# Spreading the gates' running maximum to 128 partitions through memory

## What is computed

```
x += 1/2 * post1(SwiGLU_1(pre1(x)))
x +=       postM(W_out[ mLSTM heads | S5 groups | short-conv channels ](preM(x)))
x += 1/2 * post2(SwiGLU_2(pre2(x)))
```

```
bt = cumsum(log_sigmoid(fg)); dmat[t, s] = bt[t] - bt[s] + ig[s]     (s <= t)
mt = max(max_s dmat[t, s], bt[t] + m)
w  = exp(dmat - mt);   sqk = (q k^T) * w;   num = sqk v + exp(inter - mt) * C q
```

## Time and profile before

| | before |
|---|---|
| median of the timed runs | 1109.81 us |
| the profiled execution, its own time | 1105.96 us |
| its span | 1103.2 us |
| TensorE busy | 1086.5 us (98%) |
| DVE, ACT, GpSimd busy | 536.2, 350.9, 97.6 us |
| DMA, mean | 89 GB/s |
| granted clock of TensorE, mean | 0.995 |

### The profile page before, as it was taken

One profiled execution on the slowest core, in us unless ns is written; L12 is line 12 of the kernel. 1 busy time (PEld: TensorE's weight loads), 2 busy tenths in 40 slices (PEclk: granted clock), 3 DMA queues, 4 the chain that ended last, 5 costly groups with the idle time before them and its releaser, 6 DMA issues.

```text
span 1103.2 us, 21588 instructions
## 1 busy us (share of the span) xinstructions
PE 1086.5 (98%) x8961; PEld 1069.5 (97%) x8961; DVE 536.2 (49%) x939; ACT 350.9 (32%) x517; POOL 97.6 (9%) x170
## 2 busy tenths in 40 slices
PE   8999999999999999999999899999999999999998
PEld 7999999999999999998999789999999999999997
DVE  6534433433333378864546877743333334323346
ACT  6322124221222345411535343532212222113232
POOL 0000716900000000520001000000000000000000
PEclk9999999999999999999999999999999999999999
DMA  7232322223222241222322255122323223232232
GB/s 241 91 94 77 96 78 94 88 83 96 77 81 91 72 140 32 64 75 81 115 61 61 23 111 182 40 82 90 95 77 96 78 94 91 81 96 77 85 86 82
DMA packets 32225, 97.97 MB, mean 89 GB/s; under 512 B 5800, under 2 KB 8104, under 8 KB 32168
## 3 DMA queue, kind: packets, MB, share of 16 engines
q1 hardware_dynamic: 32168, 97.17, 29.1%
HBM read 92.46 MB, written 4.70 MB: 88 GB/s over the span
## 4 chain that ended last, share of the span: by engine, by line
PE 87%; DVE 7%; ACT 3%; issue 2%; DMA 2%; SPq 0%; DVEq 0%; ACTq 0%
PE ps L1937 73%; PE ps L1962 5%; PE ps L2028 2%; PE ps L2388 2%; PE ps L2046 1%; PE ps L1969 1%; DMA raw<-w 1%; DVE x L1145 1%; DMA x<-xT 1%; ACT wh L521 1%; DVE wl L950 1%; DVE xl L1150 0%; PE ps L1974 0%; DVE y L1141 0%; DVE xl L1595 0%
## 5 line engine op out<-in xcount | busy, mean ns | idle before, releaser
L950 DVE TENSOR_TENSOR wl<-raw,wh 128x1024 fp32r<-128x1024 f32 (+1 forms) x145 | 178.5, 1231 | 458.0 <-ACT wh L521 457.6
L1937 PE MATMUL ps<-xh,wh 128*128 128x272 f32 x1616 | 336.7, 290 | 0.2 <-DVE wl L950 0.2
L1937 PE MATMUL ps<-xl,wh 128*128 128x272 f32 x1616 | 334.4, 288 | 0.0
L1937 PE MATMUL ps<-xh,wl 128*128 128x272 f32 x1616 | 333.5, 288 | 0.0
L521 ACT CAST wh<-raw 128x1024 fp32r<-128x1024 f32 (+1 forms) x145 | 150.6, 1038 | 432.3 <-PE ps L1937 429.1
L1937 PEld LDWEIGHTS ps<-xh,wh 128*128 128x128 f32 x1616 | 253.5, 189 | 1.9 <-issue 1.1
L1937 PEld LDWEIGHTS ps<-xl,wh 128*128 128x128 f32 x1616 | 254.7, 189 | 0.0
L1937 PEld LDWEIGHTS ps<-xh,wl 128*128 128x128 f32 x1616 | 253.5, 189 | 0.0
L1937 PE MATMUL ps<-hh,wh 128*128 128x272 f32 x608 | 126.3, 289 | 0.5 <-DVE hl L971 0.5
L1937 PE MATMUL ps<-hl,wh 128*128 128x272 f32 x608 | 125.5, 287 | 0.0
L1937 PE MATMUL ps<-hh,wl 128*128 128x272 f32 x608 | 125.3, 287 | 0.0
(11 more groups left out here) (466 smaller groups left out, 1191.2 us busy)
## 6 DMA issues: line engine op xcount, KB each, us to landing
raw<-w SPq DMA_DIRECT2D x118, 512.0 KB, 3.5
raw<-win SPq DMA_DIRECT2D x25, 512.0 KB, 3.5
raw<-w SPq DMA_DIRECT2D x16, 384.0 KB, 3.1
raw<-wout SPq DMA_DIRECT2D x8, 512.0 KB, 4.7
o_yT<-x SPq DMA_DIRECT2D x8, 272.0 KB, 2.2
cs<-cT SPq DMA_DIRECT2D x4, 516.0 KB, 4.4
o_sC<-cs SPq DMA_DIRECT2D x4, 516.0 KB, 7.6
x<-xT SPq DMA_DIRECT2D x3, 544.0 KB, 7.8
```

What stands on the lines that cost most here:

```text
L950: V.tensor_tensor(wl[par][:, 0:cols], raw[par][:, 0:cols], wh[par][:, 0:cols].bitcast(F32), ALU.subtract).then_inc(split_done, 1)
L1937: last = mm(ps[:, bank + s, 0:HALF], w[:, kk * P:(kk + 1) * P], a[:, kk, s * HALF:(s + 1) * HALF], start=(kk == 0 and i == 0), stop=(kk == ...
```

## The change

The four products and ACT's copy are taken out. At i = 9 SP stores the four rows of M to a buffer in device memory, `m_rows`. At i = 15, once the S5 states have been used and the store has landed, SP issues one transfer that reads the whole of this buffer (8 KB) for each of the 128 partitions of `mrow`. `exponents` waits for this transfer. The transposes of heads 0 and 1, which waited for the copy, now wait for the S5 read-out and for the copies of the gate columns.

```diff
+        mrow_in = sem("mrow_in")
+        mrow_out = sem("mrow_out")
+        m_rows = nc.dram_tensor("m_rows", (1, MH * SEQ), F32, kind="Internal").ap()
+        every = m_rows[0].partition_broadcast(P)
 ...
                     spe.dma_start(A["o_m"], row(R_E, SEQ - 1, T)).then_inc(m_out, 16)
+                    spe.dma_start(m_rows.rearrange("o (h t) -> (o h) t", h=MH), row(R_M, 0, SEQ)).then_inc(mrow_out, 16)
+                if i == 15:
+                    spe.wait_ge(hst_ready, 1)
+                    spe.wait_ge(mrow_out, 16)
+                    spe.dma_start(mrow[:].rearrange("p h t -> p (h t)"), every).then_inc(mrow_in, 16)
 ...
                 if s == 15:
-                    act.wait_ge(mb_done, 1)
-                    nc.scalar.copy(mrow[:], ps[:, 4:8, :]).then_inc(mb_evac, 1)
 ...
             def exponents():
-                dve.wait_ge(mb_evac, 1)
+                dve.wait_ge(mrow_in, 16)
 ...
-            def gate_spread():
-                pe.wait_ge(ys_evac, 1)
-                pe.wait_ge(gt_evac, 2)
-                for h in range(MH):
-                    ins = mm(ps[:, 4 + h, :], sel[0:MH, h * P:(h + 1) * P], row(R_M, 0, SEQ), start=True, stop=True)
-                ins.then_inc(mb_done, 1)
 ...
             def turn_k(h):
                 if h < 2:
-                    pe.wait_ge(mb_evac, 1)
+                    pe.wait_ge(ys_evac, 1)
+                    pe.wait_ge(gt_evac, 2)
 ...
             def turn_v(h):
                 if h < 2:
-                    pe.wait_ge(mb_evac, 1)
+                    pe.wait_ge(ys_evac, 1)
 ...
-            after = {4: [sample_bu], 8: [gate_turn], 12: [s5_y, s5_y_sample], 13: [gate_spread],
+            after = {4: [sample_bu], 8: [gate_turn], 12: [s5_y, s5_y_sample],
```

More of the change, by code:

```diff
@@ L358, in build @@
         ws_exp = sem("ws_exp")
-        mb_done = sem("mb_done")
-        mb_evac = sem("mb_evac")
+        mrow_in = sem("mrow_in")
+        mrow_out = sem("mrow_out")
+        m_rows = nc.dram_tensor("m_rows", (1, MH * SEQ), F32, kind="Internal").ap()
+        every = m_rows[0].partition_broadcast(P)
         v_done = sem("v_done")
```

## The result

The changed kernel takes 1101.5 us in the median of four runs (1100.99 to 1101.97). The kernel before has 1109.05 us in the median of its four; the ratio is 0.9936 with a 95% interval of 0.992 to 0.9951. The direction was right, the size was not. By these the first was a high draw.

A forecast was written before the change was run, and what follows sets the result against it. TensorE, busy for 98% of the span, was taken as the bound. Removing the products gave 3.7 us, and copy, waits, store and broadcast counted nothing: 1109.8 - 3.7 = 1106.1 us, range 1103.4 to 1108.7.

The forecast's parts named there:

- The copy was worth nothing by itself: ACT's 1.87 us copy from PSUM: removing it gains nothing, since ACT's next cast waits for unit 14 anyway.
- The store was free: Added issue on SP behind the small store at 466.37: over by 475, reader at 508, cost nothing.
- the bounds of 4.9 and 14.7: Broadcast from about 508.1: low and high transfer times in us, 7.0 taken; even the high end costs nothing.
- swallowed behind 585: Rival: between 585 and 640 a step tied to a transfer gives all the gain back, 1109.8 us; chance 0.06.
- The rival of the single DMA engine: Broadcast crawls on one engine, 41.5 us, delaying unit 16: slower, 1122.6 to 1125.4 us; chance 0.06.
- The estimate of 4.4 us: Broadcast time by the skill's formula: about 2.0 us fixed plus its bytes at 436 GB/s.
- The products go: Step on the four products between units 13 and 14: without them TensorE is 3.7 us shorter.
- The rival that was right: Clock rival: one slow stretch after `gate_spread` is lost too, gain 3.7 + 1.7 = 5.4 us, 1104.4 us; chance 0.10.
- that difference: Profiled execution 1105.96 us, 3.85 us below the timed runs' median of 1109.81; put on the median.
- the one with one more: Clock rival: the shift puts one more slow stretch somewhere behind, gain 2.0 us, 1107.8 us; chance 0.12.

The follow-up runs named there:

- the later traces: Traces of the nine later kernels that have the broadcast; it landed in 4.8 to 6.2 us.
- the first group: First four follow-up kernels, run on one chip beside the kernel before, whose median there was 1108.27 us (26 runs).
- the later comparisons: The changed kernel, unedited, run twice more against the kernel before: ratios 0.9956 (1102.49 us) and 0.9945 (1101.78 us).

## Why the prediction was wrong

**What held.** TensorE bounds the kernel, and what leaves its queue leaves the time. The 3.72 us of the products at full clock were right (the prediction reads the two records of each in the trace as passes of float32; that they are is not shown, and nothing hangs on it): unit 14 follows in 0.25 us, and the two profiled executions, with equal losses of clock, differ by 4.2. The copy was worth nothing by itself. The store was free, and the broadcast landed in 6.5 us for the 7.0 that I took, inside the bounds of 4.9 and 14.7 (4.8 to 6.2 in the later traces, at or near the low bound). It was issued behind DVE's signal as worked out, and its reader didn't wait. Nothing was swallowed behind 585. The rival of the single DMA engine is out: by the prediction's own estimate one engine would have needed over 40 us, and 0.93 of 16 engines were busy. Here trace and the rule of the Trainium skill (DMA: Bandwidth & Descriptors, "Why a DMA increments its semaphore by 16 and not by 1") agree; by the rule 128 partitions on both sides use all 16 engines, a repeated source row or not. The formula of the Trainium skill (DMA: Bandwidth & Descriptors, "Anatomy of one DMA") is fitted to transfers issued by GpSimd, which the prediction didn't say, and this one is issued by SP. The estimate of 4.4 us made with it is 2.1 us short of the 6.5 and 0.4 short of the shortest landing, 4.8; the measured times are what counts.

**The step that failed** is the size of the term for the products, in "The products go": "I count 3.7 us for TensorE". It is the time of the products at full clock, and it puts what they do to the clock at nothing. Their cost in the timed runs is 6.0 us (5.8 over all runs): 3.7 and 2.1 of clock by the mean of the runs. The runs showed this in four ways: the products alone take the whole gain away (0.9999 and 1.0001); products with 128 rows cost 3.1 us and leave the clock alone; eight cost 12.0 for 7.4; and the fall lies behind the products in three of five traces of kernels that have them in this place, 1.7 us each, and in none of the seven that have none, one or wide ones. By the traces alone it would be 3 / 5 x 1.7 = 1.0 us; the mean clock of the runs says 2.1. Losses ahead of 520 can't be the products', since TensorE does the same until there. From 520 on the five traces lost 3.4 us in the mean and the seven 2.2, 1.2 apart. Five traces are too few to decide between 1.0 and 2.1. I leave open how often the fall comes, and whether all of the 2.1 us lies right behind the products.

**The rival that was right** in its mechanism had a chance of 0.10: "If the change loses one that some executions had after `gate_spread`", 1104.4 us. I had seen the pattern, 4-row products in front of one fall, and let one row speak against it: that the group itself ran at 1.00. A row of one execution was taken for a property of the kernel. The same experience stood in the numbers: the timed runs lay 2 to 3.9 us above the profiled one, "about the size of one and two such stretches". I added that difference to both sides as a constant. It may have been a sign that the profiled execution had less of the thing that the change removes; its trace has no fall behind the products, but one trace can't show that this is why it was fast. The Trainium skill (TensorE: Matmul & The Clock Gate, "Part 1: The HAM clock gate") says that counts of slow matmuls vary from run to run with the kernel unchanged; the two traces of the kernel before, with losses in different places and spans of 1103.2 and 1104.7, agree. I cited it and still gave this rival 0.10.

**The range** went from the rival with one stretch less to the one with one more, 1104.4 to 1107.8, with 1 us on either side for the scatter of the times. All three stood on the single median of 1109.81. The 26 runs of the kernel before in the first group lie between 1105.92 and 1111.08, so a median of three or four is uncertain by 1 us or more. Even with the right gain of 6.0 the forecast would have been 1103.8, 2.3 above the measured 1101.5; by the later comparisons, 5.4 and 6.4 us, this remainder is such scatter. That was argued from the spread, and not tested by itself.

## What to carry to other kernels

A product on TensorE is priced by its time at full clock only if it keeps the clock up. Small products with few rows, which ran at full clock in the one execution that was profiled, can cost half as much again (6.0 us for 3.7 here) by what they do to the clock: look at several executions, and at the mean clock of the timed runs, before you price them. Where TensorE bounds the kernel and the DMA queue has cover, 20 us here, a store and a transfer that reads it for all partitions cost nothing that these runs can tell, and take the spread off TensorE. Dividing small products among wide ones has a price of its own at full clock, and a gain in clock isn't sure.

## What the runs showed of the hardware

- Behind 3.7 us of 4-row float32 products the granted clock fell to 0.50 (1.2 GHz) in three traces of five, each time with a loss of 1.7 us. Over 119 runs with them and 24 without, the time differs by 5.8 us, of which 2.1 are clock. Behind the same columns with 128 rows it didn't fall (0.9938 with and without, as the mean of 12 and 8 runs; one trace), nor behind one 4-row product of 0.9 us (one trace).
- Eight such products in a row: the clock fell to 0.50 at 528, 4.2 us after the first of them started, 5.1 us were lost in the trace, and the time rose by 12.0 us for 7.4 of work.
- Dividing the four among wide products made it worse: 5.1 us lost in the trace, 3.5 us in the time, where I had expected a gain. Dividing the other, smaller group raised the mean clock from 0.9938 to 0.9959 and left the time as it was.
- Each loss between 430 and 650, summed from neighbouring stretches, was 1.7, 3.4 or 5.1 us, in all 14 traces, and in the same kernel they lay in other places from one execution to the next.
- One 8 KB row read for 128 partitions, 1 MB in all, landed in 4.8 to 6.5 us in ten traces; in the longest, a 512 KB load had been issued 2.2 us ahead of it and another 3.7 us behind it.
